# Moving squares, norms and sample pieces between queues in a layer step on one core

## What is computed

```python
qa, ka, va, qb, kb, vb = _project(x, pos, ...)            # RMSNorm, x @ W_in, QK-norm, rotary
oa = _chunk_band_attention(qa, ka, va, A_PREV_CHUNKS, sinks, None)     # 8 heads, 2 kv heads
ob = _chunk_band_attention(qb, kb, vb, B_PREV_CHUNKS, None, rel_bias)  # 8 heads
# _merge:
oa = _rmsnorm(oa, out_norm_a)                 # 512 columns each
ob = _rmsnorm(ob, out_norm_b)
x = x + einsum('nle,ed->nld', concatenate([oa, ob]), w_out)
h2 = _rmsnorm(x, norm2)
# _hier_moe: top-1 of 4 groups, top-2 of 8 experts in it, gated MLP with 256 hidden columns
return x + _hier_moe(h2, w_rg, b_rg, w_re, b_re, w_gate, w_up, w_down)
```

## Time and profile before

| | |
|---|---|
| median of 3 runs | 939.27 us |
| profiled execution | 941.51 us |
| its span | 939.7 us |
| granted TensorE clock, mean | 0.993 of full |
| TensorE busy | 909.1 us |
| VectorE busy | 357.3 us |
| ScalarE busy | 306.0 us |

### The profile page before, as it was taken

One profiled execution on the slowest core, in us unless ns is written; L12 is line 12 of the kernel. 1 busy time (PEld: TensorE's weight loads), 2 busy tenths in 40 slices (PEclk: granted clock), 3 DMA queues, 4 the chain that ended last, 5 costly groups with the idle time before them and its releaser, 6 DMA issues.

```text
span 939.7 us, 15322 instructions
## 1 busy us (share of the span) xinstructions
PE 909.1 (97%) x6017; PEld 469.3 (50%) x6017; DVE 357.3 (38%) x962; ACT 306.0 (33%) x877; POOL 86.7 (9%) x72
## 2 busy tenths in 40 slices
PE   9999999999998999999999998898999999999995
PEld 5545545554456556566666555675333333333332
DVE  0136333234465454555555545574111111111130
ACT  2112221222426665656556546311111111111110
POOL 1000000000020000000000000002222222222111
PEclk9999999999999999999999999999999999999998
DMA  9313110111028101201101041697999999999942
GB/s 358 146 47 116 45 45 0 45 45 43 3 112 340 50 33 35 69 23 46 68 2 68 24 179 68 256 419 264 391 386 389 390 389 392 389 390 383 382 141 37
DMA packets 35157, 164.63 MB, mean 175 GB/s; under 512 B 7888, under 2 KB 9968, under 8 KB 22288
## 3 DMA queue, kind: packets, MB, share of 16 engines
q1 hardware_dynamic: 25632, 143.31, 38.2%
q0 software_dynamic: 6912, 17.32, 7.4%
q10 hardware_dynamic: 2544, 3.05, 1.0%
HBM read 147.10 MB, written 24.41 MB: 183 GB/s over the span
## 4 chain that ended last, share of the span: by engine, by line
PE 91%; DVE 5%; issue 2%; DMA 1%; ACT 1%; POOL 0%; DVEq 0%; ACTq 0%; POOLq 0%
PE ps L1464 20%; PE ps L1838 18%; PE ps L1856 9%; PE ps L1673 9%; PE ps L1482 7%; PE ps L1609 6%; PE ps L1575 5%; PE ps L1589 5%; PE ps L1821 3%; PE ps L1773 2%; DVE arena L1201 1%; PE ps L1523 1%; PE ps L1691 1%; PE ps L1638 1%; PE ps L1498 1%
## 5 line engine op out<-in xcount | busy, mean ns | idle before, releaser
L1464 PE MATMUL ps<-arena 128*128 128x512 f32 (+1 forms) x480 | 186.9, 549 | 0.0
L1838 PE MATMUL ps<-arena 128*32 128x512 f32 x1536 | 170.3, 593 | 0.8 <-ACT arena L992 0.8
L1464 PEld LDWEIGHTS ps<-arena 128*128 128x128 f32 x480 | 90.2, 189 | 92.4 <-issue 89.7
L1673 PE MATMUL ps<-arena 128*128 128x512 f32 x224 | 114.1, 594 | 0.2 <-DVE arena L1155 0.2
L1838 PEld LDWEIGHTS ps<-arena 128*32 128x32 f32 x1536 | 47.3, 109 | 105.4 <-issue 104.4
L875 ACT ACTIVATE arena<-arena 128x256 f32<-128x256 f32 (+6 forms) x144 | 83.0, 577 | 17.7 <-DVE arena L1201 17.0
L1856 PE MATMUL ps<-arena 128*32 128x512 f32 x768 | 87.0, 592 | 0.6 <-ACT arena L1015 0.6
L1120 DVE COPY arena<-ps 128x256 f32<-128x256 f32 (+2 forms) x108 | 46.8, 433 | 107.0 <-PE ps L1589 106.3
L1201 DVE CUSTOM_DVE_ANT_0 arena<-ps,arena 128x256 f32<-128x256 f32 (+6 forms) x144 | 75.0, 540 | 1.4 <-PE ps L1575 1.1
L1412 DVE SCALAR_TENSOR_TENSOR arena<-ps,arena 128x256 f32<-128x256 f32 x24 | 11.6, 485 | 160.2 <-ACT arena L1009 160.2
L1589 PE MATMUL ps<-arena 128*128 128x128 f32 (+1 forms) x400 | 64.3, 280 | 4.3 <-DVE arena L1120 1.8
(11 more groups left out here) (173 smaller groups left out, 908.9 us busy)
## 6 DMA issues: line engine op xcount, KB each, us to landing
arena<-in_wexp SPq DMA_DIRECT2D x92, 1024.0 KB, 22.2
arena<-in_x SPq DMA_DIRECT2D x18, 512.0 KB, 4.5
arena<-in_w_in SPq DMA_DIRECT2D x3, 2048.0 KB, 23.7
arena<-in_xT SPq DMA_DIRECT2D x9, 512.0 KB, 3.6
arena<-in_w_out SPq DMA_DIRECT2D x1, 4096.0 KB, 14.4
out_y<-arena SPq DMA_DIRECT2D x8, 512.0 KB, 2.6
h_rows<-arena SPq DMA_DIRECT2D x8, 512.0 KB, 3.0
arena<-in_wexp SPq DMA_DIRECT2D x8, 512.0 KB, 20.5
```

Of the source, the lines that this page charges most:

```text
L1464: ins = mm(bank(Z_BANK[c], 0, CHUNK[c]), xt[:, j, k, :], w_in[:, a:a + CHUNK[c]], start=(k == 0), stop=(k == KD - 1))
L1673: ins = mm(bank(6), turned[t % 2][:, c], w_out[:, c, 512 * n:512 * n + 512], start=(c == 0), stop=(c == KD - 1))
L1838: ins = mm(bank(s % 2)[u:u + UNIT], xgt[:, s % 2, k, u:u + UNIT], stored(expert_of(s, q), k * 512), start=(k == 0), stop=(k == KD - 1), ti ...
```

## The change

- Normed groups: ScalarE makes both squares ahead of its second copy, and the root behind that copy; each square is now linked (waits for its own completion). VectorE norms the first half ahead of `divide` and of the residual.
- The last projection piece of tile 6, group 33 slot 3, goes to group 34 slot 0.
- Group 34: the 8 chunks of the sample tile's first half are split in two times four, the second four behind `heads_back`. Group 35: its second half goes behind the scores and the turning of h2; on ScalarE the copy of the turned h2 goes ahead of the parts' copy.
- The last tile: VectorE makes the second square itself (`tensor_tensor_reduce`), counted in `s_on`. Its h2 norm of the sample tile goes first, then the divide, that square, and the copy of the logits of tile 6; `logits_out(SAMPLE - 1)` moves behind the norms. TensorE turns the sample tile's h2 into the banks 0 and 3 instead of 4 and 5, without waits for the logits between; `keep_busy(3)` goes and `keep_busy(7)` becomes `keep_busy(4)`; the two halves of the last row's transposes wait for their own norm each; the wait for `s_otv` goes into the middle of `last_out(0)`, that for `s_rv` behind it.
- One semaphore (`s_slotw`) is merged into another (`s_slot`).

```diff
--- before.py
+++ after.py
@@ -342,7 +342,7 @@
         s_ott = sem("quad_out_t_copied")
         s_ob = sem("quad_out_transposed_back")
         s_es = sem("sinks_exp")
-        s_on = sem("mixer_out_divided")
+        s_on = sem("mixer_out_divided_and_last_half_squared")
         s_so = sem("mixer_squares_summed")
         s_og = sem("mixer_out_normed")
 
@@ -376,8 +376,7 @@
         s_bx2 = sem("block_experts_in_a_row")
         s_in = sem("slot_masks_made")
         s_tab = sem("slot_tables_made")
-        s_slot = sem("slot_tokens_ready")
-        s_slotw = sem("slot_weights_ready")
+        s_slot = sem("slot_tokens_then_weights_ready")
         s_oin = sem("overflow_masks_made")
         s_otab = sem("overflow_tables_made")
         s_oslot = sem("overflow_tables_ready")
@@ -461,7 +460,9 @@
             if w == 32:
                 return {1: (6, 1, 1, 2), 2: (6, 1, 2, 3), 3: (6, 1, 3, 4), 4: (6, 1, 4, 5)}.get(slot)
             if w == 33:
-                return {1: (6, 1, 5, 6), 2: (6, 1, 6, 7), 3: (6, 1, 7, 8)}.get(slot)
+                return {1: (6, 1, 5, 6), 2: (6, 1, 6, 7)}.get(slot)
+            if w == 34:
+                return {0: (6, 1, 7, 8)}.get(slot)
             t, k = divmod(w - 6, 4)
             if not 0 <= t < SAMPLE - 1 or slot == 0:
                 return None
@@ -884,11 +885,8 @@
                     act.wait_ge(s_on, 4 * (t + 1))
                     if t >= 1:
                         act.wait_ge(s_og, 2 * t)
-                ins = nc.scalar.activation(junk[:, 512 * m:512 * m + 512], row[:, t, 512 * m:512 * m + 512], ACT.Square,
-                                           scale=512 ** -0.5, accum_out=sso[:, m:m + 1])
-                if m == 1:
-                    chain.link(ins)
-                    rstd(rso, sso).then_inc(s_so, 1)
+                chain.link(nc.scalar.activation(junk[:, 512 * m:512 * m + 512], row[:, t, 512 * m:512 * m + 512], ACT.Square,
+                                                scale=512 ** -0.5, accum_out=sso[:, m:m + 1]))
 
             def squares_row(t):
                 act.wait_ge(s_x2, 2 * (t + 1))
@@ -920,14 +918,15 @@
                 normed, squared = tile_at("normed", w), tile_at("squared", w)
                 if w >= 1:
                     heads_out(w - 1)
+                turned_out(w, 0)
                 if w == NW - 1:
                     sample_parts_out(1)
-                turned_out(w, 0)
                 copy_pt(w, 0)
                 if normed is not None:
                     squares_out(normed, 0)
+                    squares_out(normed, 1)
                     copy_pt(w, 1)
-                    squares_out(normed, 1)
+                    rstd(rso, sso).then_inc(s_so, 1)
                     copy_pt(w, 2)
                     probs(w + 1, 0)
                 elif squared is not None and squared < SAMPLE:
@@ -962,11 +961,12 @@
                 nc.scalar.activation(e12[:, t0:t1], e12[:, t0:t1], ACT.Exp).then_inc(s_v12e, 1)
 
             squares_out(LAST, 0)
-            squares_out(LAST, 1)
+            act.wait_ge(s_on, NW + 1)
+            rstd(rso, sso).then_inc(s_so, 1)
             for half in range(2):
                 act.wait_ge(s_t2, 2 * SAMPLE + half + 1)
                 nc.scalar.activation(turned[SAMPLE % 2][:, 4 * half:4 * half + 4],
-                                     bank(4 + half).rearrange("p (g c) -> p g c", g=4), ACT.Copy).then_inc(s_h2a, 1)
+                                     bank(3 * half).rearrange("p (g c) -> p g c", g=4), ACT.Copy).then_inc(s_h2a, 1)
             act.wait_ge(s_t1, 2 * LAST + 1)
             for r in range(2):
                 act.wait_ge(s_r[r], LAST - 1)
@@ -1218,11 +1218,11 @@
                 biased(w + 1, 1)
                 copy_pt(w, 1)
                 biased(w + 1, 2)
+                if normed is not None:
+                    norm_out(normed, 0)
                 if w >= 1:
                     divide(w - 1)
                 residuals(w, 1)
-                if normed is not None:
-                    norm_out(normed, 0)
                 copy_pt(w, 2)
                 if normed is not None:
                     norm_out(normed, 1)
@@ -1230,10 +1230,13 @@
                     norm_row(h2_of)
                 residuals(w, 2)
                 biased(w + 1, 3)
+            norm_row(SAMPLE)
+            divide(NW - 1)
+            dve.wait_ge(s_on, NW)
+            nc.vector.tensor_tensor_reduce(
+                out=junk[:, 512:1024], in0=row[:, LAST, 512:1024], in1=row[:, LAST, 512:1024], scale=1.0 / 512, scalar=0.0,
+                op0=ALU.mult, op1=ALU.add, accum_out=sso[:, 1:2]).then_inc(s_on, 1)
             logits_t_out(SAMPLE - 1)
-            divide(NW - 1)
-            norm_row(SAMPLE)
-            logits_out(SAMPLE - 1)
 
             dve.wait_ge(s_rload, 16 * 10)
             tt_, ts_, red = nc.vector.tensor_tensor, nc.vector.tensor_scalar, nc.vector.tensor_reduce
@@ -1328,6 +1331,7 @@
 
             norm_out(LAST, 0)
             norm_out(LAST, 1)
+            logits_out(SAMPLE - 1)
             dve.wait_ge(s_t1, 2 * NT)
             nc.vector.tensor_copy(turned[LAST % 2][:, 4:8], bank(7).rearrange("p (g c) -> p g c", g=4)).then_inc(s_otv, 1)
             logits_t_out(SAMPLE)
@@ -1358,7 +1362,7 @@
 
             dve.wait_ge(s_tab, 1)
             ts_(slot_token, bank(1, 0, NSTEP), float(FAR), None, ALU.add).then_inc(s_slot, 1)
-            nc.vector.tensor_copy(slot_weight, bank(1, NSTEP, 2 * NSTEP)).then_inc(s_slotw, 1)
+            nc.vector.tensor_copy(slot_weight, bank(1, NSTEP, 2 * NSTEP)).then_inc(s_slot, 1)
 
             def count_blocks():
 
@@ -1645,10 +1649,10 @@
                 pe.wait_ge(s_rm, 2)
                 mm(bank(6, 256, 256 + NR) if t == LAST else logits_ps, lt, sum_r, start=True, stop=True).then_inc(s_lg, 1)
 
-            def sample_parts(n):
+            def sample_parts(n, c0=0, c1=KD):
                 pe.wait_ge(s_ota, 2 * SAMPLE + 2)
                 pe.wait_ge(s_x2, 2 * SAMPLE + n)
-                for c in range(KD):
+                for c in range(c0, c1):
                     q = c % 4 * DEC
                     ins = mm(bank(6)[q:q + DEC], turned[SAMPLE % 2][:, c, 0:DEC], w_out[:, c, 512 * n:512 * n + 512],
                              start=(c < 4), stop=(c >= 4), tile_position=(0, q))
@@ -1706,11 +1710,11 @@
                 values(w - 1)
                 if routed is not None:
                     router(routed)
-                if w == NW - 1:
-                    sample_parts(1)
                 scores(w + 1)
                 rows_turned(w - 1, 1)
                 turn_rows(w, 0)
+                if w == NW - 1:
+                    sample_parts(1)
                 out_piece(w, 0)
                 if w == 0:
                     pe.wait_ge(s_tea, 2 + 2 * NT)
@@ -1723,7 +1727,7 @@
                     keep_busy(2 if w < 4 else 1, 6)
                 out_piece(w, 1)
                 if w == NW - 2:
-                    sample_parts(0)
+                    sample_parts(0, 0, 4)
                 if w == NW - 1:
                     sum_parts(1)
                 if routed is not None:
@@ -1734,6 +1738,8 @@
                 transpose_probs(w, 1)
                 if routed is None:
                     heads_back(w - 1)
+                if w == NW - 2:
+                    sample_parts(0, 4, KD)
                 if w < 6:
                     keep_busy(2 if w < 4 else 1, 6)
                 out_piece(w, 2)
@@ -1747,18 +1753,15 @@
                 out_piece(w, 4)
             values(NW - 1)
             router(SAMPLE - 1)
-            keep_busy(3)
             heads_back(NW - 1)
             pe.wait_ge(s_h2, SAMPLE + 1)
-            pe.wait_ge(s_lt, SAMPLE)
-            turn_h2(SAMPLE, 0, 4)
+            turn_h2(SAMPLE, 0, 0)
+            turn_h2(SAMPLE, 1, 3)
             turn_logits(SAMPLE - 1)
-            pe.wait_ge(s_rv, SAMPLE)
-            turn_h2(SAMPLE, 1, 5)
-            keep_busy(7)
-            pe.wait_ge(s_og, 2 * NT)
+            keep_busy(4)
             pe.wait_ge(s_x2, 2 * LAST)
             for half in range(2):
+                pe.wait_ge(s_og, 2 * LAST + half + 1)
                 for c in range(4):
                     k = 4 * half + c
                     ins = nc.tensor.transpose(bank(6 + half, c * P, c * P + P), row[:, LAST, k * P:k * P + P], ident)
@@ -1766,7 +1769,6 @@
             keep_busy(3)
             router(SAMPLE)
             pe.wait_ge(s_ota, 2 * LAST + 1)
-            pe.wait_ge(s_otv, 1)
 
             def last_out(n, c0=0, c1=KD):
                 for c in range(c0, c1):
@@ -1779,7 +1781,10 @@
                         ins = mm(ps[:, t * NE:t * NE + NE], tri if s == t else ones, mb[:, s], start=(s == 0), stop=(s == t))
                 return ins
 
-            last_out(0).then_inc(s_op, 1)
+            last_out(0, 0, 4)
+            pe.wait_ge(s_otv, 1)
+            last_out(0, 4, KD).then_inc(s_op, 1)
+            pe.wait_ge(s_rv, SAMPLE)
             turn_logits(SAMPLE)
             last_out(1, 0, 4)
```

(2 more changed lines are left out.)

## The result

The changed kernel takes 931.16 us (median of 4 runs, 931.03 to 932.05) against 939.68 us (939.19 to 940.54) of the kernel before beside it: a ratio of 0.991, 95% interval 0.9898 to 0.9922, or 8.5 us less. 930.8 us had been forecast, with 928.8 to 934.4 as the range. The profiled execution has a span of 929.3 us where the old one had 939.7; that difference of 10.4 is larger than that of the medians, and why is a part of this story.

What follows compares the result with a forecast made beforehand. TensorE, busy 97% of the span, was taken as the bound, so only dropped work or closed idle time could win. Gains of 3.0 + 1.3 + 4.2 = 8.5 us off the median 939.27 gave 930.8 us, range 928.8 to 934.4.

Steps and rivals of the forecast that it cites:

- Part 1: Normed groups: squares ahead of the copy and norm ahead of the divide remove TensorE's waits for the norm; gain 3.0 us.
- Part 2: Sample tile's pieces, groups 33 to 35: moved pieces cover TensorE's waits for copies; gain 1.3 us, bounds 0.6 and 1.6.
- Part 3: Last tile, behind group 35: less filler and squares on two engines start transposes at 597.0, not 600.96; gain 4.2 us.
- (a): Tail behind group 35: TensorE's clock falls again, losing 1.7 us, to 932.5; chance 0.20.
- (b): First normed group: the clock stays up during its transposes, winning another 1.0 us, to 929.8; chance 0.10.
- (c): Sample tile's moves bring nothing, as VectorE's residual ahead of the copy stops it and TensorE: 932.1 us; chance 0.11.
- (d): Behind the routing: the gathers meet the expert loads and lose 3.4 us, to 934.2; chance 0.06.
- (e): Low clock over longer work: 10 us of it turns the gain into -1.5, 940.8 us; chance 0.03.
- (f): Start of the experts: held by something else, a load or table, so the gain becomes a wait: 939.3 us; chance 0.03.

Runs made afterwards that it cites:

- e4: The changed kernel with the last projection piece of tile 6 left in group 33, slot 3: 931.03 us, ratio 0.9916.
- e2: The kernel before with only the moves of the sample tile's pieces in groups 33 to 35: 938.93 us, ratio 0.9989.
- e6: The kernel before with only VectorE's norm put ahead of the divide, ScalarE's squares as before: 939.45 us, ratio 0.9993.
- e1: The kernel before with the new order in the normed groups alone, squares first and norm ahead of the divide: 936.18 us, ratio 0.9957.
- e3: The kernel before with only the changes behind group 35, the last tile's: 936.05 us, ratio 0.9957.
- e8: The changed kernel with the old filler, keep_busy(3) back and 7 instead of 4: 933.26 us, ratio 0.992.
- e9: The kernel of e4 with the first normed group in the old order on ScalarE and VectorE: 931.2 us, ratio 0.9903.
- e5: The kernel before, unchanged, profiled a second time: 941.61 us, span 939.8.
- e7: The kernel before with only less filler behind group 35, keep_busy(3) away and keep_busy(7) cut to 4: 939.35 us, ratio 0.9996.

## Why the prediction was right, and where it wasn't

**Part 1** held in mechanism and was mis-sized a little. Full groups: 0.74 each where I took 0.6 to 0.7; the two middle ones 0.65 and 0.63 where I took 0.46 to 0.55; the second 0.23 against 0.2. The term left out each time was what lies between the modelled end of a piece and the start of what follows without a wait (0.87 from start to start, where the piece is shown with 1.02). Five groups of this kind and the second give 3.7, against 3.0 in the sum, which had been taken from the lower part of its own 2.9 to 3.4. The first group was foretold with 0, bounds -0.4 and 0.2; measured against traces with the clock up it is -0.3 (1.20 against 1.53), for a reason that I had half: the late statistic holds VectorE's queue, not the late copy TensorE. Group 33, put at 0, gave 0.19.

**Part 2** was foretold with 1.3, bounds 0.6 and 1.6, and is 0.3: outside. The step that failed is "does half of the sample pieces, turns probabilities at 576.8 instead of 577.7". I had put the residual of tile 6 behind the moved piece and asked only which copies of VectorE it delays. But `sample_parts(0)` itself waits for that residual (`s_x2` at 14), since it writes bank 6 from which the residual reads. In the old order the residual was done by 572.3 and this wait was never seen, so no row named it; with the piece moved it is 0.39 us, and group 34 keeps nothing. e4 shows it: the move undone, 0.46 comes back. I had read the order of the queues where the code of the wait had to be read. The other third of the miss is in group 35, 0.37 where the sum had 0.7: the transposes gain 0.95 there, but the sum of the parts follows them by 0.96 us instead of 0.49, for ScalarE's copy of the parts (0.30 of wait), and the prediction had let it give back 0.3 only.

**Part 3** was foretold to the row: 597.0 in the old frame for the transposes, measured 591.76 + 5.23 = 596.99; the projection 4.2 earlier, measured 4.20; the second square, taken at 0.75, is 0.69 and 0.08 for its sum; the statistic, the norms and the wait of 1.0 (0.95) for the logits are within 0.2 of where they were put. But the 4.2 is counted from a profile with the low clock in it, and 1.65 of it belong to that (e2, e6). From an execution without it the same change gives 2.55. The sum was then taken off the median, which lies 2.2 under that profile, and this is a step that isn't sound: a gain that is partly "no low clock" can only be taken off an execution that has one.

**Why the number came out.** Two cuts through the executions show the change without the clock. The shortest are 938.07 before and 931.03 after, 7.0 apart. The mean granted clock gives the other: in the twelve traces it is 0.995 or 0.996 where no low stretch stands ahead of the one that closes every trace, and 0.993 or 0.994 where one or two do. Of 57 executions of the kernel before, 20 had 0.995 or more, and their median is 938.94, 7.8 over that of the changed kernel, of which all four had it.

By the traces it is 3.9 up to group 35 (the row "after" gives 5.4 against the old trace, and 1.53 of that the old code gives by itself when the clock stays up) plus 2.55 behind it, 6.4. The remaining 0.6 to 1.4 is not traced to the change. What varies between the traces is the first gather (4.28 to 5.77 us) and the last scatter, the DMA that adds the experts' last rows to y (6.0 to 7.3 us from issue to landing). It took 7.3 in the old trace and 6.2 in the new one, which is the 1.07 by which the spans' 10.4 exceeds the 9.36 of the last expert matmul; the change doesn't touch it, and why it differs isn't shown. The medians are 8.5 apart, since the runs of before spread up to 943.21 and those of after end at 932.05. Four runs of the changed kernel are few; the six of e1, whose tail is the old one, lie from 935.9 to 936.48 with a mean clock of 0.994 or 0.995, those of e3 from 934.98.

Does the new order in the tail meet the low clock less often? In front of the last projection none of five traces with it has a low stretch, and five of seven with the old order do. But three of the five (e3, e8, e9) have one some 25 us later, where it costs 1.4 all the same, and e6 of the others has one later still; counted over the whole way to the experts' first steps it is three of five against six of seven. The executions say more: 22 of 29 with the new tail had a mean clock of 0.995 or more, against 30 of 104 with the old one. This is a count, not a mechanism that I isolated. So between 0.7 and 1.5 of the 8.5 us are the clock's.

Part 1 gave 0.6 more than foretold (3.7, plus 0.19, less 0.3, against 3.0), part 2 gave 1.0 less and part 3 by itself 1.65 less: the three terms come to 6.4 instead of 8.5. That 931.16 still lies 0.4 from the forecast is luck: the clock and what isn't traced made up the 2.1.

**Rivals.** (a), the clock falls in the tail again, did not happen in the profile, though e3, e8 and e9 show it behind the projection, at 1.4 each. (b), the clock recovers in the first group, happened in the trace, but as chance: the same code runs either way (e2 against e5), and with the idle time split the clock fell in e8, so the split is neither needed for it nor enough. (c) is what part 2 came to: nearly nothing, by the residual, only through a wait of TensorE itself. (d) cost 0.1 (4.70 against 4.62). (e) and (f) did not happen; the expert stage shifted whole, by 9.35 us at its first step and 9.36 at its last. The Trainium skill's rule in "TensorE: Matmul & The Clock Gate", section "Part 1: The HAM clock gate", that activity releases the throttle, agrees with the traces in part only. The falls in the first group and behind group 35 came after idling of TensorE, but the same 1.20 us of idling was followed by a clock of 1.00 (e2) and of 0.50 (e5), with fewer filler calls the changed kernel kept 1.00, and in e9 the clock fell at 620 behind 2.00 us of busy time in 2.00.

## What to carry to other kernels

Ask of each wait not only who ended it, but what would be late next: of the two moves here one gave 0 alone, the other 0.36, and both 0.74. When a piece of work is moved past a wait, read the waits of the code that now follows it, those too that the trace never shows because they were long satisfied; a shared PSUM bank is such a one. Filler in front of a matmul that others wait for becomes the limit itself when the clock is low (eighteen instructions took 3.87 us instead of 2.24). Where the granted clock of a profile shows low stretches, cost them by themselves and take several executions, the shortest of each kernel beside the medians, before a gain in that stretch is called the change's.

## What the runs showed of the hardware

The low level of TensorE's clock (0.50 of full, 1.2 of 2.4 GHz) came and went between executions of the same instructions behind the same idle time: groups 5 and 6 took 1.5 us longer in the earlier trace rows and e5 than in e2, e3 and e7. The stretches that could be priced cost 1.4 to 1.65 us each, wherever they fell, and an execution of the kernel before took 938.07 to 943.21 us: a spread of 5 us, more than any single part of this change. VectorE's 128x512 square with its sum out of SBUF took 0.69 us plus 0.08 for the read, ScalarE's 0.63 plus 0.19, so two engines side by side saved about 0.6 us against two on one.
